# Two transformer blocks on one core: the split weight tiles change their place in SBUF, and the per-stage buffers begin 96 bytes further on

## The reference

```python
# first block
h = modulate(rmsnorm(x, norm1_g), shift1, scale1)      # shift, scale, gate: silu(c) @ ada_w + ada_b
z = h @ w_in + b_in                                    # 1024 x 2048
y = concat(rmsnorm(spatial_gating(gelu(u), gelu(v))), rmsnorm(conformer_conv(val, gate)))
x = x + gate1 * (y @ w_out)
h2 = modulate(rmsnorm(x, norm2_g), shift2, scale2)
g_ff, up_ff = split(h2 @ w_ffn_in)                     # 1024 x 5632
x = x + gate2 * ((silu(g_ff) * up_ff) @ w_ffn_out)     # 2816 x 1024
# second block, two layers: attention (8 forgetting heads, 8 sparse heads), then a pooling mixer
for layer in (0, 1):
    m = mixer(rmsnorm(h))                              # layer 0 ends in "concat(o_fox, o_nsa) @ w_out"
    h = h + rmsnorm(m)
    h = h + rmsnorm(swiglu(rmsnorm(h)))                # again 1024 x 5632, then 2816 x 1024
```

## The kernel before

| tiles | first byte | past a multiple of 128 |
|---|---|---|
| `raw` 0 to 3 | 16,512 | 0 |
| `w_hi` 0, 1, `w_lo` 0, 1 | 39,040 to 61,568 | 0 |
| `x_res` | 61,568 | 0 |
| `h_hi`, `h_lo` (and `h_scratch`) | 77,952 and 94,336 | 0 |
| `tmp`, `tmp2`, vectors | 110,720 | 0 (`ident`, `ones`: 96) |
| `hid_hi`, `hid_lo`, `m_out` | 122,016, 167,072, 212,128 | 32 |
| `ao_hi`, `ao_lo` | 122,016, 138,400 | 32 |
| `c_rows`, `p_t`, `w1b`, q, k and v tiles | from 122,016 on | 32 |
| `ada_acc`, `y_shifted`, `ada_w` | 178,880, 187,072, 212,672 | 64 |

## Time and profile before

### The profile page before, as it was taken

The page is one execution under the profiler, slowest core; times in us unless marked ns, Lnnn a source line. Parts: engine busy times, 40 slices in busy tenths (PEclk is TensorE's granted clock), DMA queues, the critical chain, the costliest instruction groups (busy, mean ns, idle before and its releaser), DMA issues.

```text
span 1837.0 us, 22013 instructions
## 1 busy us (share of the span) xinstructions
PE 1716.6 (93%) x8143; PEld 1339.8 (73%) x8143; DVE 898.1 (49%) x1334; ACT 661.1 (36%) x949; POOL 189.4 (10%) x186
## 2 busy tenths in 40 slices
PE   1999899999999959999999899999999899999996
PEld 1657678888888737766666688888887688888885
DVE  6765584533322262356556744444335744444223
ACT  1324334444322241455555444443223433333221
POOL 4001119910000060000000000000200000000000
PEclk9999889999999969999999899999998799999998
DMA  7564154522322232111101132223222032223221
GB/s 280 206 193 160 44 186 165 178 103 91 116 83 94 73 58 82 58 35 37 45 24 57 58 102 92 97 98 117 95 74 79 13 101 94 94 100 113 95 78 46
DMA packets 49112, 179.73 MB, mean 98 GB/s; under 512 B 5985, under 2 KB 6657, under 8 KB 48929
## 3 DMA queue, kind: packets, MB, share of 16 engines
q1 hardware_dynamic: 44896, 166.75, 26.9%
q0 software_dynamic: 3008, 10.59, 2.1%
q10 hardware_dynamic: 1152, 1.66, 0.3%
HBM read 173.56 MB, written 2.10 MB: 96 GB/s over the span
## 4 chain that ended last, share of the span: by engine, by line
PE 67%; issue 21%; DVE 8%; ACT 1%; POOL 1%; DMA 1%; ACTq 1%; POOLq 0%; DVEq 0%; SPq 0%
PE bank L328 16%; PE bank L329 15%; PE bank L330 15%; PE bank L1167 3%; PE bank L1169 2%; PE bank L1168 2%; PE bank L1227 2%; PE bank L1271 2%; PE bank L1247 2%; DVE ada_acc L1631 1%; PE bank L1325 1%; PE bank L1152 1%; DVE tmp L513 1%; DMA raw<-in_ada_w 1%; PE bank L410 1%
## 5 line engine op out<-in xcount | busy, mean ns | idle before, releaser
L267 DVE TENSOR_TENSOR w_lo<-raw,w_hi 128x1024 fp32r<-128x1024 f32 (+1 forms) x236 | 322.5, 1367 | 679.1 <-ACT w_hi L263 678.8
L328 PE MATMUL bank<-h_hi,w_hi 128*128 128x512 f32 x1248 | 495.1, 397 | 7.0 <-DVE h_lo L506 3.5
L329 PE MATMUL bank<-h_lo,w_hi 128*128 128x512 f32 x1248 | 488.2, 391 | 0.0
L330 PE MATMUL bank<-h_hi,w_lo 128*128 128x512 f32 x1248 | 488.1, 391 | 0.0
L263 ACT ACTIVATE w_hi<-raw 128x1024 fp32r<-128x1024 f32 (+1 forms) x236 | 265.3, 1124 | 574.2 <-PE bank L330 506.8
L328 PEld LDWEIGHTS bank<-h_hi,w_hi 128*128 128x128 f32 x1248 | 235.6, 189 | 70.6 <-issue 11.3
L330 PEld LDWEIGHTS bank<-h_hi,w_lo 128*128 128x128 f32 x1248 | 235.6, 189 | 49.9
L329 PEld LDWEIGHTS bank<-h_lo,w_hi 128*128 128x128 f32 x1248 | 235.9, 189 | 47.6 <-issue 1.0
L328 PE MATMUL bank<-hid_hi,w_hi 128*128 128x512 f32 x528 | 209.7, 397 | 0.0
L329 PE MATMUL bank<-hid_lo,w_hi 128*128 128x512 f32 x528 | 209.5, 397 | 0.0
L330 PE MATMUL bank<-hid_hi,w_lo 128*128 128x512 f32 x528 | 209.5, 397 | 0.0
(11 more groups left out here) (313 smaller groups left out, 1899.0 us busy)
## 6 DMA issues: line engine op xcount, KB each, us to landing
raw<-in_f2i SPq DMA_DIRECT2D x88, 512.0 KB, 3.2
raw<-in_ffi SPq DMA_DIRECT2D x44, 512.0 KB, 3.2
raw<-in_f2o SPq DMA_DIRECT2D x32, 704.0 KB, 4.0
ada_w<-in_ada_w SPq DMA_DIRECT2D x32, 512.0 KB, 4.1
raw<-in_att_w SPq DMA_DIRECT2D x24, 512.0 KB, 3.2
raw<-in_ffo SPq DMA_DIRECT2D x16, 704.0 KB, 4.0
raw<-in_ada_w SPq DMA_DIRECT2D x16, 512.0 KB, 5.1
raw<-in_w_in SPq DMA_DIRECT2D x16, 512.0 KB, 5.3
```

The lines of the kernel that those rows point to most:

```text
L267: nc.vector.tensor_tensor(WL[par][:, 0:kc * P], RAW[s][:, 0:kc * P], WH[par][:, 0:kc * P].bitcast(F32), ALU.subtract).then_inc(wlo, 1)
L328: pe_.matmul(bank[:, :], w_h, hi[:, k0 + k, :], start=start and k == 0, stop=False)
L329: pe_.matmul(bank[:, :], w_h, lo[:, k0 + k, :], start=False, stop=False)
L330: last = pe_.matmul(bank[:, :], w_l, hi[:, k0 + k, :], start=False, stop=stop and k == kc - 1)
```

## The change

The lines that allocate the four split weight tiles move from behind `raw` to behind PAD, and PAD grows from 21 to 45 float32 values (from 84 to 180 bytes, which take up 96 and 192). No instruction is added, removed or moved on any engine or queue: only addresses differ.

```diff
         RAW = [sb(f"raw{i}", [P, KH * P]) for i in range(4)]
-        WH = [sb(f"w_hi{i}", [P, KH * P], F32R) for i in range(2)]
-        WL = [sb(f"w_lo{i}", [P, KH * P], F32R) for i in range(2)]
         X = sb("x_res", [P, C, S])
...
         NS, RB, RB2 = PS[6], PS[7], PS[5]
-        PAD = sb("pad_to_row", [P, 21])
+        PAD = sb("pad_to_row", [P, 45])
+        WH = [sb(f"w_hi{i}", [P, KH * P], F32R) for i in range(2)]
+        WL = [sb(f"w_lo{i}", [P, KH * P], F32R) for i in range(2)]
```

## The result

The changed kernel takes 1845.02 us, the median of 7 runs (1844.34 to 1850.35); the kernel before, on the same chips, 1836.5 us (1833.92 to 1840.86, 7 runs). The ratio is 1.0053 with a 95% interval of 1.0042 to 1.0063: 0.5% slower. I had forecast 1827.4 us and a range up to 1833.5.

A forecast was written before the change was run, and what follows sets the result against it. The prediction took the rate of TensorE's successive matmuls as the bound. Gains of 10.5 + 1.3 + 0.1 = 11.9 us off 1838.76 us gave 1826.9, or 1827.4 us with the median's 0.58 us added; range 1822.5 to 1833.5 us.

The forecast's parts named there:

- That TensorE's rate is the time: Whole kernel: TensorE busy 1716.6 of 1837.0 us, so the rate of successive matmuls sets the time; savings come off the end.
- The gain on `hid_*` and `ao_*`: Narrow phases and attention output: moving tiles brought to a multiple of 128 save 6.67 ns a matmul, 10.5 and 1.3 us.
- the term for the moved weights and `h_*`: Weight tiles and wide-phase moving tiles: place relative to a multiple of 128 is kept, so effect taken as 0.
- upper memory: Rival: surcharge belongs to memory above byte 122,000, so it stays on `hid_*` and `ao_*`; 1839.3 us, no-effect chance 0.06.
- The slow rival: Weights above the moving tile slow 4320 matmuls on `h_*` to 233.3 ns, 28.8 us more; 1856.2 us, chance 0.04.
- Plain float32 matmuls, VectorE, ScalarE at 0: About 1240 plain float32 matmuls and the VectorE and ScalarE instructions: indifferent to the new start addresses, 0 us.
- Nothing at half clock: Start of ffo0: at 1.2 GHz steps take 426 ns without surcharge, so 11 matmuls are left out of the gain.

The follow-up runs named there:

- e2: Kernel before with 32 bytes put in front of the weight tiles and taken from PAD, all these tiles at 160 modulo 512; 1826.01 us, ratio 0.994.
- e4: Changed kernel with PAD back at 21 values, so only the weight tiles move against the kernel before; 1851.03 us, ratio 1.0076 to the kernel before.
- e1: Kernel before with PAD at 45 values alone, weight tiles left below h_hi; 1834.78 us, ratio 0.9985.
- e3: Changed kernel with 128 bytes put in front of x_res and taken from PAD; 1825.72 us, ratio 0.9941 to the kernel before.
- s1: Kernel before with 64 bytes in front of x_res and PAD at 64 values; one execution, 1830.28 us against 1837.82.
- t1: From e2, with h_lo alone 32 bytes further and hid_hi and hid_lo read from 16 bytes further; 1849.22 us against 1838.84 for the kernel before.
- s4: Kernel before with 160 bytes in front of x_res and PAD at 56 values; one execution, 1859.32 us against 1837.82.
- s2: Kernel before with 96 bytes in front of x_res and PAD at 40 values; one execution, 1859.86 us against 1837.82.
- t2: From e2, with gaps putting w_lo alone at 128 modulo 256, the other tiles at 160; 1847.92 us against 1838.84 for the kernel before.

## Why the prediction was wrong

- *That TensorE's rate is the time* was right: the gain and loss of each phase went through to the end, in every timed run.
- *The gain on `hid_*` and `ao_*`*, 10.5 and 1.3 us, was right in size: 9.9 and 1.0 us in the profile after, 3.5 us in each of ffo1 and ffo2 and 3.0 in ffo0, where 13 steps instead of 10 ran at 426 ns. Its cause was wrong, and the size was right by luck: the same 96 bytes took the tiles to a multiple of 128 and, with the weights' move, to distance 0. I read the 16 cycles as one more 64-byte piece for a tile off its multiple. e2 and e4 run at 226.7 ns on tiles 32 bytes past a multiple of 128, and e1 at 232.4 to 233.3 ns on tiles at one.
- *The step that failed* is the term for the moved weights and `h_*`: "These keep their place relative to a multiple of 128; only the absolute address and the neighbours differ. I take 0". It measured 20.2 us. The right reference was the other tile and 256 bytes: the distance of `h_*` from the weights went from 38,912 bytes (152 x 256) to -44,160 bytes, which is 128 more than a multiple of 256. The same subtraction for `hid_*`, 82,976 before (32 over) and 22,528 after (88 x 256), would have named both effects from the two tables of addresses.
- *The wrong inference from good rows.* The trace before had two groups of tiles that differed in two things at once, the offset to 128 and the distance to the weights. I wrote down offset and upper memory as the possible causes and did not list the distance. I also held against the other causes that the surcharge was fixed at 16 cycles "to the accuracy of the timeline"; only the mean over many steps is, single ones are 6 ns apart, 230 to 236 ns between 540 and 634 us.
- *The slow rival* had the right direction and place, `h_*` slowed by where the weights went, at 28.8 us instead of 20.2: 6.67 ns a matmul instead of at most 5.7, and 576 more matmuls, of which the 384 at L1167 to L1169 paid 0.3 us together and the 192 of the two helpers none that can be told from their changes of clock. Its mechanism, weights above or next to the moving tile, fell in e3. My argument against it, VectorE writing `tmp` beside `h_lo`, spoke of another engine's writes, and those indeed cost nothing that the steps show (232.4 ns with and without).
- *Plain float32 matmuls, VectorE, ScalarE at 0* held. The lines of the kernel after that answer to the earlier trace rows:

```profile
L1008 PE MATMUL bank<-y_shifted,conv_w_tiles x192: 592/592/617, 88.3 to 138.3; 128*32 128x512 f32 x192
```

```profile
L674 DVE TENSOR_TENSOR tmp<-bank,m_out 128x512 f32<-128x512 f32 x44 | 30.1, 683 | 0.0
L683 DVE TENSOR_TENSOR hid_lo<-tmp,hid_hi 128x512 f32 x40 | 27.7, 692 | 36.6 <-ACT hid_hi L665 36.6
L665 ACT ACTIVATE hid_hi<-tmp 128x512 f32 x40 | 25.3, 632 | 108.4 <-DVE tmp L681 108.4
```

- *Nothing at half clock* held too. The start of ffo0 after shows 426 ns steps at a granted clock of 0.50, as in the earlier trace rows, now at distance 0 (the last row has PE, weight loads, VectorE, ScalarE and GpSimd, then clock, DMA share and GB/s):

```profile
518.33 0.63 PE L329 MATMUL bank<-hid_lo,w_hi 128*128 128x512 f32 x1
...
522.60 0.63 PE L330 MATMUL bank<-hid_hi,w_lo 128*128 128x512 f32 x1
...
518.00:522.00 4.00, 4.00 (x10) 3.13 (x11) 1.51 (x4) 0.48 (x1) 0.00 (x0) 0.50 0.51 180
```

What stays open is the mechanism inside. The runs show that the step of the float32r matmuls hangs on the distance between moving and weight tiles modulo 256 bytes, with the other engines idle as with them busy; that the moving read and the weight load meet in the memory is the reading that is left, not seen itself. The runs do not show which weight load would meet which read, nor why some distances settle into two different rates.

## What to carry to other kernels

Where float32r matmuls follow each other at full clock, place moving and stationary tiles so that their first bytes agree modulo 256. (Chunks and weight pieces lie 2048 and 512 bytes apart here, multiples of 256; another step was not tried, but it would change the distance from chunk to chunk.) It took 0.6% off this kernel (e2, e3); each of the two versions compared had it in some stages only. When a rate differs between two groups of tiles, list every way in which their addresses differ, relative to each other too, before choosing a cause; and move one tile alone before moving several.

## What the runs showed of the hardware that I had not expected

The step of a 128x128 by 512 float32r matmul at full clock, by the distance from both weight tiles to the moving tile modulo 256 bytes, in the phases of the feed-forward networks:

| distance | step, ns | seen at |
|---|---|---|
| 0 | 226.7 | before and e1 (`h`), after, e4 and s1 (`hid`), e2, e3 (all) |
| 16 | 231.7 | t1 (`hid`), start not tried apart |
| 32 | 233.3 | before (`hid`) |
| 64 | 228.9, 233.3 in one phase | s1 (`h`), s4 (`hid`) |
| 96 | 233.3 | s2 (`h`) |
| 128 | 232.4 to 233.3 | after (`h`), e1 (`hid`) |
| 160 | 234.3 | s4 (`h`) |
| 192 | 233.3 | s2 (`hid`) |
| 224 | 233.3 | e4 (`h`) |

Distance 0 gave 226.7 ns in every such phase, whether the tiles lay at remainders of 128, 160 or 256 modulo 512; no other distance gave it in any.

The Trainium skill says otherwise in "SBUF — State Buffer", section "Who interferes with whom": its table gives TensorE two independent read ports, one for the moving operand and one for LDWEIGHTS. Whatever the ports are, the place of the one operand to the other counts in these runs: t2 changed the distance of `w_lo` alone against e2 and the steps rose from 226.7 to between 231.0 and 232.5 ns. By the cachelines of 16 bytes in the box of that page's section on Door 1 a shift of 16 bytes should also be free; t1 measured 231.7 ns.
